# One more pair of gate tiles ahead of attention, and attention's rows turned three steps after their logits

## The reference, cut to what matters

```
h = x + 0.5 * SwiGLU_1(RMSNorm(x))
u = RMSNorm(h)
[xp | q | k | v | gate_logits] = u @ w_in        # 512 | 512 | 512 | 512 | 2 * 1024 columns
y_pool = causal_pool_mixer(xp) @ w_branch_pool
y_sb   = stick_breaking_attention(q, k, v) @ w_branch_attn     # 8 heads of 64
m = sigmoid(g_pool) * y_pool + sigmoid(g_sb) * y_sb
h = h + m @ w_out
h = h + 0.5 * SwiGLU_2(RMSNorm(h))
out = RMSNorm_final(h)
```

## Time and profile before

| | |
|---|---|
| median of three runs | 1917.43 us (1917.35 to 1917.62) |
| profiled execution, its own time | 1918.11 us |
| its span, first to last instruction | 1916.2 us |
| PE busy | 1903.5 us (99%), 9010 matmuls |
| DVE busy | 1372.2 us (72%) |
| ACT busy | 796.4 us (42%) |
| POOL busy | 115.9 us (6%) |
| DMA | 348.24 MB, mean 182 GB/s |
| mean granted clock of TensorE | 0.999 |

### The profile page before, as it was taken

One profiled execution on the slowest core, in us unless ns is written; L12 is line 12 of the kernel. 1 busy time (PEld: TensorE's weight loads), 2 busy tenths in 40 slices (PEclk: granted clock), 3 DMA queues, 4 the chain that ended last, 5 costly groups with the idle time before them and its releaser, 6 DMA issues.

```text
span 1916.2 us, 24977 instructions
## 1 busy us (share of the span) xinstructions
PE 1903.5 (99%) x9010; PEld 1592.0 (83%) x9010; DVE 1372.2 (72%) x1677; ACT 796.4 (42%) x1175; POOL 115.9 (6%) x157
## 2 busy tenths in 40 slices
PE   9999999999999999999999999999999999999998
PEld 8888888888888888888888888898888888888887
DVE  6978777784566776488677768889777777756555
ACT  7423232323434544234676752474323232324344
POOL 1000000000000300000233220010000000000001
PEclk9999999999999999999999999999999999999999
DMA  5456654558676733416875447643545444677665
GB/s 165 144 198 230 223 181 140 199 189 306 208 240 201 195 110 132 132 50 181 226 174 148 128 139 260 197 138 119 178 144 196 149 169 153 216 264 244 206 192 206
DMA packets 258419, 348.24 MB, mean 182 GB/s; under 512 B 29344, under 2 KB 161184, under 8 KB 255008
## 3 DMA queue, kind: packets, MB, share of 16 engines
q1 hardware_dynamic: 258336, 347.15, 56.3%
HBM read 233.83 MB, written 112.99 MB: 181 GB/s over the span
## 4 chain that ended last, share of the span: by engine, by line
PE 97%; DVE 1%; DMA 1%; issue 0%; SPq 0%; ACT 0%; POOL 0%; POOLq 0%; DVEq 0%; ACTq 0%
PE bank L1263 40%; PE bank L1372 9%; PE bank L1319 9%; PE bank L1321 9%; PE bank L1320 9%; PE bank L1513 6%; PE bank L1215 3%; PE bank L1449 2%; PE bank L1421 2%; PE bank L1479 2%; PE bank L1585 2%; PE bank L1604 1%; PE bank L1190 1%; PE bank L1603 1%; PE bank L1570 1%; PE bank L1568 1%
## 5 line engine op out<-in xcount | busy, mean ns | idle before, releaser
L2253 DVE TENSOR_TENSOR dn_lo<-dn_lo_raw,dn_hi 128x1024 fp32r<-128x1024 f32 x149 | 181.9, 1224 | 149.6 <-ACT dn_hi L1788 149.1
L1263 PE MATMUL bank<-lo_t,wa_hi 128*128 128x512 f32 x656 | 252.8, 389 | 0.0
L1263 PE MATMUL bank<-hi_t,wa_hi 128*128 128x512 f32 x656 | 252.8, 389 | 0.0
L1263 PE MATMUL bank<-hi_t,wa_lo 128*128 128x512 f32 x656 | 252.8, 389 | 0.0
L1788 ACT ACTIVATE dn_hi<-dn_lo_raw 128x1024 fp32r<-128x1024 f32 x149 | 158.0, 1061 | 218.8 <-DMA dn_lo_raw<-act_dram 218.8
L1319 PE MATMUL bank<-dn_hi 128*128 128x512 f32 x596 | 232.7, 390 | 0.0
L1321 PE MATMUL bank<-dn_lo,dn_hi 128*128 128x512 f32 x596 | 231.9, 389 | 0.0
L1320 PE MATMUL bank<-dn_hi,dn_lo 128*128 128x512 f32 x596 | 231.9, 389 | 0.0
L1263 PE MATMUL bank<-hi_b,wa_hi 128*128 128x512 f32 x492 | 190.6, 389 | 1.0 <-DVE up L2387 1.0
L1263 PE MATMUL bank<-lo_b,wa_hi 128*128 128x512 f32 x492 | 190.5, 389 | 0.0
L1263 PE MATMUL bank<-hi_b,wa_lo 128*128 128x512 f32 x492 | 190.4, 389 | 0.0
(11 more groups left out here) (275 smaller groups left out, 3747.7 us busy)
## 6 DMA issues: line engine op xcount, KB each, us to landing
wa_lo_raw<-in_ffn_w_gate_up_dram SPq DMA_DIRECT2D x87, 512.0 KB, 5.0
dn_lo_raw<-act_dram SPq DMA_DIRECT2D x149, 256.0 KB, 4.2
act_dram<-g SPq DMA_DIRECT2D x44, 512.0 KB, 4.4
wd_t<-in_ffn_w_down_dram SPq DMA_DIRECT2D x44, 512.0 KB, 6.6
act_dram<-s_of SPq DMA_DIRECT2D x88, 256.0 KB, 6.5
wd_dram<-wd_t SPq DMA_DIRECT2D x22, 1024.0 KB, 6.0
dn_lo_raw<-wd_dram SPq DMA_DIRECT2D x85, 256.0 KB, 3.4
dn_lo_raw<-in_ffn_w_down_dram SPq DMA_DIRECT2D x64, 256.0 KB, 3.0
```

The costliest lines, as they stand in the source:

```text
L1263: last = nc.tensor.matmul(acc, lhs, rhs, start=n == 0 and i != 2 and i < 5, stop=n == 11, skip_group_check=True)
L2253: return nc.vector.tensor_tensor(dst, raw, hi.bitcast(f32), ALU.subtract)
```

## The change

- `EARLY` goes from 4 to 6. The attention gates of tiles 4 and 5 are made in a third gate unit among the mix units, and the gate units inside attention are five in place of six: three of two pool gates each, two of one pool and one attention gate each.
- Tiles are turned three steps after their logits (`LAG`) in place of two, and weighed one step later, at odd steps; rows have a fourth place (a3), where the two pool rows were, which move. The loop has 69 steps in place of 68.
- VectorE always takes the low half of the turned tile ahead of the scan.
- The five drain steps have a share of 12 each, in place of four with 7.
- Values of the next pair of heads are split in steps 12, 13 and 14, in place of 11, 12 and 16. Pieces of gate unit 1 are split later.
- SyncE issues gate unit 1 and the first two pool rows after head 0's loads; output loads are spread over five steps.
- The second plain projection uses banks 4 to 7, and the slots of the branch weights change parity with the number of gate units.

```
-EARLY = 4
+EARLY = 6
-DRAIN = 4
-V_DIFF, V_HIGH, V_LOW = ({NT + 3 + d: 1, 3 * NT + 3 + d: 2, 5 * NT + 3 + d: 3} for d in (0, 1, 5))
+DRAIN = 5
+LAG = 3
+V_DIFF, V_HIGH, V_LOW = ({NT + 4 + d: 1, 3 * NT + 4 + d: 2, 5 * NT + 4 + d: 3} for d in (0, 1, 2))
-    shares = [SHARE[x["qt"]] for x in TILES] + [7] * DRAIN
+    shares = [SHARE[x["qt"]] for x in TILES] + [12] * DRAIN
-    return gate_step(piece_start(j) + (7 + 18 * piece if j < NG - 1 else 1 + 6 * piece))
+    return gate_step(piece_start(j) + (26 if j == 1 else 7) + (16 if j == 1 else 18) * piece if j < NG - 1 else piece_start(j) + 1 + 6 * piece)
-        pool_y = at("pool_y", [P, 2, HALF], f32, G0)
+        pool_y = at("pool_y", [P, 2, HALF], f32, o + 16384)
+        a3 = at("a3", [P, SEQ], f32, G0)
...
             gate_unit(0)
             spill_pool_branch(2)
-            gate_unit(1)
...
             load_head(0)
+            sp_.wait_ge(y_even_sp, 16)
+            load_pool_y(0)
+            sp_.wait_ge(y_sp[1], 16)
+            load_pool_y(1)
+            gate_unit(1)
             spill_pool_branch(3)
             load_head(1)
...
-            load_pool_y(0)
-            load_pool_y(1)
             gate_unit(2)
...
-                return a2[:, :] if n % 3 == 2 else a[:, n % 3, :]
+                return (a[:, 0, :], a[:, 1, :], a2[:, :], a3[:, :])[n % 4]
...
-                if s >= 4 and s % 2 == 0:
-                    weigh((s - 4) // 2)
-                if 2 <= s < NA + 2:
-                    turn(s - 2)
+                if s >= LAG + 2 and s % 2:
+                    weigh((s - LAG - 2) // 2)
+                if LAG <= s < NA + LAG:
+                    turn(s - LAG)
...
-                if n >= 3:
-                    act.wait_ge(t_ok, CHUNKS[n - 2])
+                if n >= 4:
+                    act.wait_ge(t_ok, CHUNKS[n - 3])
...
-                turned_first = 2 <= s <= NA and TILES[s - 1]["qt"] in (1, 5, 3)
-                if turned_first:
-                    turned_lo(s - 2)
+                if LAG <= s < NA + LAG:
+                    turned_lo(s - LAG)
                 if 1 <= s <= NA:
                     weigh_keys(s - 1)
-                if 2 <= s < NA + 2 and not turned_first:
-                    turned_lo(s - 2)
```

More of the change, by code:

```diff
@@ L1106, in _ @@
                         store_gate(fb)
-                    if s == NA:
+                    if s == NA + 1:
                         move_o(NA // 2 - 2, 3, slice(0, HALF // 2))
-                    elif s == NA + 2:
+                    elif s == NA + 3:
                         move_o(NA // 2 - 1, 4, slice(HALF // 2, HALF))
-                    elif s >= 4 and s % 2 == 0:
-                        store_o((s - 4) // 2)
+                    elif s >= LAG + 2 and s % 2:
+                        store_o((s - LAG - 2) // 2)
                     if s == O_STEP:
@@ L1116, in _ @@
                             sp_.wait_ge(o_sp[b], 32 * (NA // 4 - 2))
[L1117 to L1120, removed]
+                    if O_STEP <= s < O_STEP + 5:
+                        load_output(s - O_STEP, slice(0, P if s < O_STEP + 3 else 64))
                     if s == NA:
@@ L1382, in unit_quad @@
                     th, ab = b // 2, b % 2
-                    wait_bank(b, q)
+                    if not fresh:
+                        pe.wait_ge(tr_free, 4 * NT)
                     cols = slice(th * HALF, (th + 1) * HALF)
@@ L1388, in unit_quad @@
                     for part in range(2):
-                        last = products(bank[:, b, :], par, ab, lambda kt: u_hi[:, kt, cols],
+                        last = products(bank[:, b if fresh else 4 + b, :], par, ab, lambda kt: u_hi[:, kt, cols],
                                         lambda kt: u_lo[:, kt, cols], part=(part * 12, part * 12 + 12))
@@ L1486, in mix_unit @@
             def mix_unit(b):
-                s = (b + 1) % 2
+                s = (b + NM + 1) % 2
                 for i in range(7):
                     place, hi, lo, (kind, slot) = PRODUCTS[i]
[L1491 to L1494, removed]
+                    if b < 2 and i in (0, 1, 3, 4):
+                        wait_bank(place, Q_A[b] + 1)
                     if b >= 2 and i == 0:
@@ L1945, in take_first @@
                 act.wait_ge(acc_ready, 4 * Q_A[m] + b + 1)
-                nc.scalar.activation(ring_hi[n % 3][:, th * HALF:(th + 1) * HALF], bank[:, b, :], ACT.Copy,
+                nc.scalar.activation(ring_hi[n % 3][:, th * HALF:(th + 1) * HALF], bank[:, 4 * m + b, :], ACT.Copy,
                                      scale=1.0 if ab else QSCALE).then_inc(ev_hi, 1)
@@ L1969, in mix_first @@
                 act.wait_ge(mb_prod, 7 * b + 1)
-                nc.scalar.activation(mix_dst(b, 0, 0), bank[:, 4 * ((b + 1) % 2), :], ACT.Copy).then_inc(mb_copied, 1)
+                nc.scalar.activation(mix_dst(b, 0, 0), bank[:, 4 * ((b + NM + 1) % 2), :], ACT.Copy).then_inc(mb_copied, 1)
             def mix_second(b):
@@ L1976, in mix_second @@
                     act.wait_ge(mb_add, 5 * b)
-                nc.scalar.activation(mid[:, :], bank[:, 4 * ((b + 1) % 2), :], ACT.Copy).then_inc(mb_copied, 1)
+                nc.scalar.activation(mid[:, :], bank[:, 4 * ((b + NM + 1) % 2), :], ACT.Copy).then_inc(mb_copied, 1)
             def mix_post(b, a, th, adds):
@@ L2202, in _ @@
             for s in range(NA + DRAIN):
[L2203 to L2206, removed]
+                if s >= LAG + 2 and s % 2:
+                    take_o((s - LAG - 2) // 2)
+                if LAG <= s < NA + LAG:
+                    turned_hi(s - LAG)
                 if s < NA:
@@ L2690, in take_first @@
                 cols = slice(th * HALF, (th + 1) * HALF)
-                nc.vector.scalar_tensor_tensor(out=ring_lo[(2 * m + ab) % 3][:, cols], in0=bank[:, b, :], scalar=1.0 if ab else QSCALE,
+                nc.vector.scalar_tensor_tensor(out=ring_lo[(2 * m + ab) % 3][:, cols], in0=bank[:, 4 * m + b, :], scalar=1.0 if ab else QSCALE,
                                                in1=ring_hi[(2 * m + ab) % 3][:, cols].bitcast(f32), op0=ALU.mult,
@@ L2755, in mix_c11 @@
                 dst = mix_dst(b, 0, 0)
-                nc.vector.tensor_tensor(dst, bank[:, 4 * ((b + 1) % 2) + 1, :], dst, ALU.add).then_inc(mb_add, 1)
+                nc.vector.tensor_tensor(dst, bank[:, 4 * ((b + NM + 1) % 2) + 1, :], dst, ALU.add).then_inc(mb_add, 1)
             def mix_c22(b, part):
-                dst, s = mix_dst(b, 1, 1), (b + 1) % 2
+                dst, s = mix_dst(b, 1, 1), (b + NM + 1) % 2
                 if part:
@@ L3119, in split_branch @@
                 dve.wait_ge(whi, U_C + j + 1)
-                dst, raw, hi = (flat(w[:, j % 2, 0, 0:BR]) for w in (w_lo, w_raw, w_hi))
+                dst, raw, hi = (flat(w[:, (U_C + j) % 2, 0, 0:BR]) for w in (w_lo, w_raw, w_hi))
                 nc.vector.tensor_tensor(dst, raw, hi.bitcast(f32), ALU.subtract).then_inc(wlo, 1)
```

19 lines of the change are left out of this document (10 added, 9 removed).

## The result

The change made the kernel slower: 1922.68 us median of 9 runs (1921.63 to 1924.76) against 1917.61 (1916.87 to 1918.09) in the same comparison. The ratio is 1.0028, with a 95% interval of 1.0019 to 1.0037. The forecast was 1914.8, in a range up to 1918.2. The profiled execution took 1924.76 us, with a span of 1922.9.

The account below looks back on a forecast made before the run. TensorE's queued work was taken as the bound, busy 1903.5 of 1916.2 us. Matmuls minus 2.8, start minus 1.3 plus 1.5, lag 0 sum to minus 2.6: 1914.8 us from the median 1917.43, eight in ten between 1912.8 and 1918.2.

Parts of the forecast that it names:

- Matmuls, -2.8: TensorE: 84 matmuls (19.04 us) added before attention, 96 (21.98 us) taken from it; net minus 2.8 us.
- The start, -1.3 and +1.5: Start of attention: k wait falls to about 0.3, gain 1.3 us; spills behind gate unit 1 cost a 1.5 us wait.
- the late bound: Start of attention: spills land at 923.0 at the latest, making TensorE wait 3.0 us before tile 1's turn.
- Lag, zero net: Attention, turn three steps after logits: 0.7 us put for two tight places equals the waits that go; zero net.
- the bound of 0.7: Lag term in attention: bounded by minus 0.7 and plus 1.5 us.
- the two tightest places: Low halves between the 1024- and 896-wide turns (fits by 0.13 us) and of the 384-wide tile (about 0.5).
- Values, nothing: Values split in steps 12 to 14 of a head pair: same three instructions where only short scans follow, no cost.
- the 19.04 us of the mixer: Mixer stretch: the added mix unit makes it 19.0 us longer, with TensorE still fully busy.
- the end: End of attention: 43 gate matmuls, 9.8 us, after the last product with the values, without a wait.
- Gate unit 1's pieces and the output loads: Attention: later pieces (steps 2, 4, 7, 9) and output loads spread over five steps cost nothing.
- The third rival: Attention: shorter steps make VectorE's order the bound, GpSimd stretching scans; 1921.8, or 1918.3 in half the heads; chance 0.13.
- the prediction's own signs: Wrong if over 2 us of low-half or scan waits after first head, added-mix-unit waits, or attention shorter by under 20.

Follow-up runs that it names:

- three repairs: Changed kernel with gate unit 1 ahead of head 0's loads, values' low half in step 16, last gate unit's pieces nine matmuls apart: 1915.98 us.
- the best kernel with six tiles: Kernel with three repairs and the larger first step, but the last gate unit's pieces six gate matmuls apart again: 1913.75 us, ratio 0.9981.
- the larger first step: HEAD_SHARE 28 in place of 16 on the kernel with three repairs, 19 gate matmuls in the first step in place of 13: 1914.65 us.

## Why the prediction was wrong

The runs put side by side, medians in us:

| | 4 early tiles | 6 early tiles | difference |
|---|---|---|---|
| as changed | 1918.77 | 1922.68 | +3.9 |
| three repairs | 1915.63 | 1915.98 | +0.4 |
| repairs, HEAD_SHARE 28 | 1913.81 | 1914.65 | +0.8 |

Predicted for the difference: -2.8. The +0.4 and +0.8 are not told from zero (the best kernel with six tiles, 1913.75, is level with the best with four), but in no pair did the 2.8 us come. Predicted for everything else: +0.2 (the start); measured +1.2 (1918.77 less 1917.57), a loss of 3.1 that the repairs take back less a gain of 1.9. The sum was -2.6 and came out at +5.1 in its own comparison: of these 7.7 us the difference column has 6.7 and the rest 1.0.

**Matmuls, -2.8.** This is the step that failed most. The arithmetic was right, but 96 matmuls were priced at their own time, as if they covered nothing. The added unit took 19.04 us as predicted. For attention I took the distance between TensorE's starts from the timeline: for a gate matmul 0.2267 us is undisturbed, for the other pairs of kinds the shortest tenth; the rest is stall. Undisturbed work is 229.1 us with four tiles as changed and 207.3 with six, 21.8 less. The stretch itself became 13.2 us shorter as changed, and 18.3 with the repairs and the larger first step, both less than 19.04. Table by stretches, four tiles as changed, then four and six tiles with the repairs and the larger first step:

```profile
909.38:1151.02 241.64, 237.40 (x1377) 205.29 (x1376) 167.27 (x200) 159.60 (x372) 89.19 (x80) 1.00 0.62 168
909.01:1145.63 236.62, 236.13 (x1377) 205.69 (x1376) 166.03 (x200) 159.69 (x372) 92.37 (x80) 1.00 0.62 168
928.49:1146.81 218.32, 216.47 (x1282) 186.45 (x1280) 162.36 (x196) 155.61 (x364) 85.05 (x79) 1.00 0.64 172
```

So 96 matmuls fewer open 8.6 us of stalls as changed and 3.5 with the repairs. Of the 8.6, half lies at the start: the waits there are 4.54 in place of 1.94 us, and 1.7 are the slow clock. Another 3.0 are longer waits for low halves later on, and 1.4 are in no list of waits. (The profiled executions lie 5.7 us apart, the medians 3.9, so some 1.8 of the 8.6 is theirs.) Of the 3.5, 1.1 are in the lists and 2.4 are not. A pause under 0.17 us shows in no list, since a record of 0.39 us covers it where the next start is due after 0.2267; what TensorE stood for in these is not shown.

**The start, -1.3 and +1.5.** The gain of 1.3 failed: the k wait was 1.85, not 0.3. Without the 1 MB in front the last k_lo load, issued at 928.60, was put at the 2.7 us of a quiet stretch and took 4.1, against 4.64 in the earlier trace rows; with the 1 MB in front again it took 3.3 (DMA issues, changed kernel and gate unit 1 ahead):

```profile
k_lo<-qk_dram SPq DMA_DIRECT2D x1, 128.0 KB, 4.1
```

```profile
k_lo<-qk_dram SPq DMA_DIRECT2D x1, 128.0 KB, 3.3
```

The spill wait was 2.69 in the profile, inside its bounds, but that was luck: the spills landed later than the late bound, 14.9 us into attention (943.05) where it was 13.7 (923.0), because issuing them took 6.26 us in place of 2.25, and the late k made TensorE late as well. The drop of the clock behind a pause was not in the sum; either the k pause or the spill pause brings it. Putting gate unit 1 back gave 1.8 us. The Trainium skill (DMA: Bandwidth & Descriptors, Queues, rings and completion order) has the descriptors of a ring consumed in ring order, though a later one may finish its write before an earlier one; by the order of consumption the spills come after the gate unit. The trace agrees: the gate unit's two loads had landed at 940.42, the four spills by 943.05.

**Lag, zero net.** At four early tiles the lag and what goes with it gained 1.9, outside the bound of 0.7; at six the kernel is 11.2 slower with the old lag, places and order. It was priced by the two tightest places, while it moves every head's. How much of either number is the lag's own is not shown.

**Values, nothing.** This failed by 2.8 us. "Only short scans follow" looked at what is behind the instruction; what counted was what stands between it and the low half that TensorE needs next, and the change had moved that low half behind it.

**Right:** the 19.04 us of the mixer and the end (43 matmuls in 9.83 us, no wait). Gate unit 1's pieces and the output loads show no cost. The third rival had the side, and with VectorE's order as the bound a part of the mechanism, at 1918.3 to 1921.8; in the changed kernel its place was another, and the start, which the rest came from, was no part of it. By the prediction's own signs, over 2 us of low-half waits after the first head (5.2 here) and attention shorter by under 20 us were to show it wrong, and did.

Open: why three repairs together give 1.7 us more than singly, which is no more than an interval, and what the start costs in a typical execution, since each profile shows one.

## What to carry to other kernels

Where matmuls without dependences fill the gaps of a tightly ordered stage, taking some away is not worth their own time: count the gaps that they cover, small ones and waits for transfers alike, and try the same change at the old amount of filler before crediting the exchange. When a helper's instruction is moved, look at which result of that helper comes next on the path, under the new order, not at what was behind it under the old. A threshold in a schedule (a bank finished one step sooner) can put an engine's wait ahead of urgent work: 24 matmuls in place of 23 in the first step of the kernel before cost some 8 us here (1926.55 against 1918.18).

## What the runs showed of the hardware

- One pause of TensorE of 1.96 us for k, and one of 1.98 in another kernel, were followed by a granted clock of 0.50; one of 1.85 us at the same place was not, nor one of 1.61 us in the kernel before. Two pauses of 1.13 and 0.77 us, 1.1 us apart, left it at 1.00. After pauses of 2.69 and 5.98 us it fell too.
- Issuing the same four 256 KB spills took SyncE 2.25 us in the kernel before, where gate unit 1 stands ahead of head 0, and 6.26, 4.79, 5.23 and 5.11 us behind head 0, the pool rows and gate unit 1 (four kernels with that order); in the runs with the gate unit ahead of head 0 again it was 2.2 to 2.5 us. The issuing itself is slower in that order, and all that follows in SyncE's list starts later.
- A 640-wide scan of VectorE took 2.37 us beside a GpSimd product that began 0.25 us before it, and 1.48 us in two places without one.
